# Splitting the first weight block of the projections as well, so that its second unit runs in split passes

## The reference, cut to what matters

```
D_MODEL = 1024; SEQ = 256
(dq, dk, dv, dz, da, db, aq, ak, av, gate_dn, gate_da) = split_columns(xn @ w_in[layer], IN_WIDTHS)
...
q, kc, vc, ks, vs, kw, vw, gl = jnp.split(h @ w_in, cuts, axis=-1)      # NSA
return o @ w_out                                                        # NSA, out of the mixer
...
q, f, i, g = jnp.split(h @ w_in, [HGRN_F_DIM, 2 * HGRN_F_DIM, 2 * HGRN_F_DIM + D_MODEL], axis=-1)   # HGRN2
return o.reshape(b, t, D_MODEL).astype(h.dtype) @ w_out                 # HGRN2, out of the mixer
```

## The kernel before

| call | starts near | units |
|---|---|---|
| first input projection (DeltaNet) | 23 us | 3 blocks feature, 2 token (the last 16 columns wide) |
| second input projection (dilated attention) | 250 us | 6 feature, 3 token |
| NSA in | 1210 us | 6 token (the last 48 columns wide) |
| NSA out (`out_projection`) | 1429 us | 2 token |
| HGRN in | 1809 us | 4 feature, 4 token |
| HGRN out (`out_projection`) | 1994 us | 2 token |

## Time and profile before

### The profile page before, as it was taken

One profiled execution on the slowest core, in us unless ns is written; L12 is line 12 of the kernel. 1 busy time (PEld: TensorE's weight loads), 2 busy tenths in 40 slices (PEclk: granted clock), 3 DMA queues, 4 the chain that ended last, 5 costly groups with the idle time before them and its releaser, 6 DMA issues. The chain is left out here.

```text
span 2366.2 us, 27792 instructions
## 1 busy us (share of the span) xinstructions
PE 2097.6 (89%) x10752; PEld 1413.5 (60%) x10752; DVE 1420.5 (60%) x2421; ACT 610.1 (26%) x1010; POOL 464.9 (20%) x402
## 2 busy tenths in 40 slices
PE   7889998998997777777789898899999978899998
PEld 6679897774542222222257885566775866566584
DVE  5455553557888888555574466433666667443394
ACT  1411102422111111000010231333652052233372
POOL 1032000104443333334312001100011033100000
PEclk9889999999999999999998899999999999999999
DMA  5830664539999999999957101889996532589997
GB/s 206 305 108 1 215 214 147 213 108 419 393 421 421 421 422 421 421 421 418 398 191 213 41 1 47 338 352 355 394 377 241 200 137 73 208 348 351 352 409 283
DMA packets 142432, 650.98 MB, mean 275 GB/s; under 512 B 17976, under 2 KB 22736, under 8 KB 97084
## 3 DMA queue, kind: packets, MB, share of 16 engines
q1 hardware_dynamic: 94012, 354.09, 39.6%
q0 software_dynamic: 46336, 291.93, 30.2%
q10 hardware_dynamic: 1952, 3.18, 0.5%
HBM read 642.46 MB, written 16.85 MB: 279 GB/s over the span
## 5 line engine op out<-in xcount | busy, mean ns | idle before, releaser
L1840 PE MATMUL psum<-peer_uv_rows,peer_weight_diagonal 128*128 128x512 f32 x932 | 453.2, 615 | 108.4 <-DVE peer_weight_diagonal L1966 108.1
L1840 PEld LDWEIGHTS psum<-peer_uv_rows,peer_weight_diagonal 128*128 128x128 f32 x932 | 161.8, 190 | 390.6 <-DVE peer_weight_diagonal L1966 264.9
L1973 DVE SCALAR_TENSOR_TENSOR peer_uv_rows<-peer_uv_rows,peer_x 128x1024 f32<-128x1024 f32 x233 | 285.5, 1225 | 143.6 <-DMA peer_uv_rows<-peer_uv,peer_index 141.3
L1794 POOL DMA_INDIRECT peer_uv_rows<-peer_uv,peer_index x233 | 241.8, 1038 | 448.2 <-PE psum L1840 332.0
L147 DVE TENSOR_TENSOR moe_weight_parts<-weight_ring,moe_weight_parts 128x2048 fp32r<-128x2048 f32 x80 | 182.6, 2290 | 156.4 <-ACT moe_weight_parts L2858 156.0
L1873 ACT ACTIVATE peer_gelu<-peer_dots 128x1 f32<-128x1 f32 x256 | 51.5, 202 | 548.7 <-DVE peer_uv_rows L1973 497.4
L2858 ACT ACTIVATE moe_weight_parts<-weight_ring 128x2048 fp32r<-128x2048 f32 x80 | 152.1, 1911 | 38.0 <-DMA weight_ring<-moe_w 26.1
L153 PE MATMUL psum<-moe_weight_parts,moe_block_x_parts 128*128 128x512 f32 x352 | 142.6, 405 | 11.7 <-DVE moe_block_x_parts L147 7.2
L154 PE MATMUL psum<-moe_weight_parts,moe_block_x_parts 128*128 128x512 f32 x352 | 139.6, 397 | 0.0
L155 PE MATMUL psum<-moe_weight_parts,moe_block_x_parts 128*128 128x512 f32 x352 | 139.4, 396 | 0.0
L2977 POOL DMA_INDIRECT h_t<-moe_tokens,moe_block_tokens x30 | 36.9, 1232 | 498.5 <-PE psum L2676 411.0
(11 more groups left out here) (565 smaller groups left out, 3996.8 us busy)
## 6 DMA issues: line engine op xcount, KB each, us to landing
weight_ring<-moe_w SPq DMA_DIRECT2D x76, 2048.0 KB, 10.3
weight_ring<-ada_w SPq DMA_DIRECT2D x24, 2048.0 KB, 9.2
moe_weight_ring_end<-moe_w SPq DMA_DIRECT2D x20, 2048.0 KB, 12.3
weight_ring<-w_in SPq DMA_DIRECT2D x17, 2048.0 KB, 9.4
weight_ring<-hgrn_w_in SPq DMA_DIRECT2D x8, 2048.0 KB, 9.5
moe_results<-moe_block_out POOLq DMA_DIRECT2D x26, 512.0 KB, 10.3
weight_ring<-nsa_w_in SPq DMA_DIRECT2D x5, 2048.0 KB, 7.9
weight_ring<-peer_wq SPq DMA_DIRECT2D x4, 2048.0 KB, 8.1
```

The lines of the kernel that those rows point to most:

```text
L1794: nc.gpsimd.indirect_dma_start(buffer(t), None, S.dram["peer_uv"], bass.IndirectOffsetOnAxis(ap=experts[:, t:t + 1], axis=0)).then_inc(row ...
L1840: last = nc.tensor.matmul(S.ps[:, 2 * a + c, :], diag[:, t % 4, :], v_rows(t)[:, c * BANK:(c + 1) * BANK], start=(i == 0), stop=(i == PICK ...
L1973: nc.vector.scalar_tensor_tensor(u_rows(t), u_rows(t), 1.0, x2[:, t // PICKS, :], ALU.mult, ALU.mult, accum_out=dots[:, t:t + 1]).then_inc ...
```

## The change

Block 0 keeps its first unit plain and runs its second unit (i = 1) split. PE's waits for the split parts move there: for `split_made` 1 and 2 and for `x_split` 1 and 2 at k = 0 and k = 4 of unit 1. DVE parts block 0 ahead of block 1. If unit 1 is a feature unit, only the columns that it uses are parted (`first = width // 2`), so an instruction is 128x4x256; otherwise the whole block is. The counts of `masked` and `split_made` are two higher for every later block, and as block 0 now has room in `wp` too, `split_block(2)` waits for `spent` 1.

```diff
                 def product(out, k, lhs_part, rhs_part, fresh):
-                    if not with_parts or b == 0:
+                    if not with_parts or i == 0:
                         return nc.tensor.matmul(out, lhs_part(lhs, w), rhs_part(lhs, w), start=(k == 0), stop=(k == K - 1))
                     if fresh and k % (K // 2) == 0:
-                        pe.wait_ge(split_made, 2 * b + k // (K // 2) - 1)
-                        if b == 1:
+                        pe.wait_ge(split_made, 2 * b + k // (K // 2) + 1)
+                        if b == 0:
                             pe.wait_ge(x_split, k // (K // 2) + 1)
...
-                    fresh = w is None
+                    fresh = w is None or i == 1
...
-                    if b >= 3:
+                    if b >= 2:
                         dve.wait_ge(spent, b - 1)
+                    first = width // 2 if b == 0 and units[1][0] == "feature" else 0
                     for h in range(2):
-                        part = half(h, k * width)
-                        high_part(nc, high[:, part], w[:, part]).then_inc(masked, 1)
-                        dve.wait_ge(masked, 2 * b + h - 1)
-                        low_part(nc.vector, low[:, part], w[:, part], high[:, part]).then_inc(split_made, 1)
+                        part = lambda y: y[:, 0:k * width].rearrange("p (k n) -> p k n", k=k)[:, half(h, k), first:width]
+                        high_part(nc, part(high), part(w)).then_inc(masked, 1)
+                        dve.wait_ge(masked, 2 * b + h + 1)
+                        low_part(nc.vector, part(low), part(w), part(high)).then_inc(split_made, 1)
...
                     if b == 1:
                         dve.wait_ge(spent, 1)
-                    dve.wait_ge(split_made, 2 * b)
+                    dve.wait_ge(split_made, 2 * b + 2)
                     dve.sem_inc(S.w.used, 1)
                 if with_parts:
+                    split_block(0)
                     split_block(1)
```

## The result

| | kernel before | changed kernel |
|---|---|---|
| timed runs, median | 2369.58 us (20 runs) | 2376.52 us (20 runs) |
| lowest to highest | 2365.91 to 2373.06 | 2370.47 to 2383.86 |
| ratio, 95% interval | | 1.0030 [1.0022, 1.0038] |
| span of the profiled execution | 2366.2 us | 2369.7 us |

The change makes the kernel slower by 7 us, 0.3%. The profiled execution of the changed kernel was one of its quick ones: 2371.5 us in all, 1.8 us more than its span and 5.0 under the median. With the same 1.8 us on top, the profiled execution of the kernel before took about 2368.0 us (an estimate), 1.6 under its median. So the two spans differ by 3.5 us only, and a comparison of the two traces can explain the six calls, but not all of the 7 us; the last experiments are about that.

What follows compares the result with a forecast made beforehand. PE was taken to set each call's end, with DVE close behind and stretched by POOL. Gains of 0.14, 1.16 and 0.17 against losses of 1.81, 2.07 and 1.8 made +4.2 us on 2370.98, so 2375.2 us, range 2370 to 2381.

Steps and rivals of the forecast that it cites:

- the 0.2% bound: About 0.2% (4.7 us) is what a measurement can tell from no change; the forecast, 0.18% slower, lay within it.
- the likeliest single case: The main forecast, slower but staying within 0.2% of the kernel before; chance 0.44.
- PE's side: Six calls: a plain unit becomes split, saving 1.16 us per feature call and 1.43 per token call, 7.8 if PE never waits.
- DVE's side: Extra splitting on DVE: 6.93 us per token call, 3.72 us for the half block in feature calls.
- rival 3: Feature calls: narrow split saves nothing, CAST of 4x256 taking 1.22 us; 2377.2 us, or 2381.7 with both at full length; chance 0.06.
- The turns with POOL: DVE and POOL block each other, so POOL adds 4.3 us to DVE's chain in whichever order they go.
- Rival 1: DVE is in time: POOL's 4.3 us don't lengthen the chain, no call waits, 7.8 us gained, 2363.2 us; chance 0.10.
- The waits: PE waits for DVE's parts: three per token call (1.6 to 1.9, then twice 0.7 us), one in first call and HGRN in.
- NSA out: Token call: unit 3's mover starts at 1455.62 instead of 1453.55, 2.07 us lost.
- Rival 2: Clock falls in the token calls' new waits, each of three calls paying 1.7 us; 2380.3 us; chance 0.13.
- Rival 4: The waits don't come about, PE or DVE starting otherwise in token calls; gains and losses near nothing, 2371 us; chance 0.04.
- the sum: Six calls: -0.14 - 1.16 - 0.17 + 1.81 + 2.07 + 1.8 = +4.2 us, later stages passing it on unchanged.

Runs made afterwards that it cites:

- the last experiments: Four kernels repeated on another chip (changed kernel 1.0045, feature calls alone 1.0015), then waits padded into the kernel before (0.9999) and decay-table loads moved first in the changed kernel (1.0029).
- both series: The first runs, and a second set of four kernels run together on another chip: kernel before against itself 1.0007, changed kernel 1.0045.

## Why the prediction was right, and where it wasn't

The time, 2376.52 us, lies in the range, 1.3 us over the forecast of 2375.2. But the kernel before measured 2369.58 this time and not 2370.98, so the loss was 6.9 us where +4.2 was forecast: slower by more than the 0.2% bound, where the likeliest single case was just within it.

**PE's side** held: 6.91 to 5.75 in the second call, with no wait, because DVE starts on the half block as soon as block 0 is there, while block 1 is still loading.

**DVE's side** held. On the line between the two known widths the half block had 3.72 us; the third and fourth of its instructions in the second call, away from POOL, run from 255.96 to 257.81, 1.85 us a half where 1.86 was read off the line:

```profile
255.96 0.68 DVE L142 CAST project_weight_parts<-weight_ring 128x1024 fp32r<-128x1024 f32 x1
256.67 1.23 DVE L147 TENSOR_TENSOR project_weight_parts<-weight_ring,project_weight_parts 128x1024 fp32r<-128x1024 f32 x1
257.81 1.22 DVE L142 CAST project_weight_parts<-weight_ring 128x2048 fp32r<-128x2048 f32 x1
```

With this rival 3 is out: CAST takes 0.68 and not 1.22.

**The turns with POOL** held: 4.3 us in whichever order. The second and third instruction in NSA in pay 2.07 and 2.17 beyond the 2.29 and 1.22 that they take alone. In the first call, where the narrow instructions go first, TENSOR_TENSOR at 24.00 pays nothing and the two behind it 2.2 and 2.0. The run without POOL's work shows the cause by taking it away. Rival 1 was right in what follows from a shorter chain (3 us less was its deciding point, and with 4.2 less nothing waits), and wrong in that this kernel isn't there: POOL does lengthen the chain.

**The waits** came where they were said to be, eleven of them. The profile gives 1.45, 0.54 and 0.40 us where 1.6 and twice 0.7 were worked out, but the two count differently. The matmuls ahead follow each other every 0.23 us and are shown as 0.39 long, so PE's pace is interrupted for 0.16 us more than the idle time in the brackets: 1219.61 - 1217.78 - 0.23 = 1.60 for the first, some 0.7 and 0.56 for the others. Only the third is short, by 0.14, because the slow start behind one wait is taken out of the next and the prediction counted it only behind the last. The end isn't touched by this, because only the last wait sets it: 1226.54 + 0.11 for the slow start + 8.16 + 0.22 = 1235.03, where the mover stands.

**NSA out** was mis-sized by 0.25: +2.07 against +1.82. I took the end of DVE's chain in the kernel before, 1437.83 + 2.29, as given, but there DVE began 0.3 us after ScalarE. Its first instruction before, then after:

```profile
1428.92 1.23 DVE L142 CAST project_weight_parts<-weight_ring 128x2048 fp32r<-128x2048 f32 x1 [0.61 <-DVEq L1355]
```
```profile
1427.38 1.23 DVE L142 CAST project_weight_parts<-weight_ring 128x2048 fp32r<-128x2048 f32 x1 [0.32 <-PEq L1357]
```

In the changed kernel it began 0.02 us after ScalarE. An engine's own start at a stage belongs to the measurement, not to the chain.

**Rival 2** is out. The clock in the three stretches with the new waits, of NSA in, NSA out and HGRN out:

```profile
1216.00:1226.00 10.00, 8.02 (x34) 5.79 (x32) 9.90 (x6) 0.04 (x1) 0.14 (x1) 1.00 0.00 0
1435.00:1445.00 10.00, 8.02 (x34) 5.86 (x32) 9.90 (x6) 0.00 (x0) 0.23 (x1) 1.00 0.00 0
2003.00:2013.00 10.00, 7.61 (x32) 5.33 (x31) 9.90 (x7) 0.00 (x0) 0.00 (x0) 1.00 0.00 0
```

PE stood for a fifth to a quarter of these stretches and was granted 1.00 throughout, and so it was to the end of the three calls. **Rival 4** is out too: the waits came.

**What the sum left out** stands in the last sentence before it, "All later stages begin when the call ends, so gains and losses pass on". It puts everything outside the six calls at nothing, and there the timed runs lost some 3 us more than the calls did. By the line through all runs of both series some 2.5 us go with a lower mean clock, and 1.3 us don't and have no known place but for 0.3. Those belong to the small load that lands late in the convolution stage, which was in no term either; of its 1 us only 0.3 are left at the stage's end: from the start of the first call to the start of the stage behind the convolution it is 87.85 us before and 87.80 after, so most of that call's 0.16 is gone. The range covered all this, as "the spread of the runs", without any of it being foreseen. That the time came within 1.3 us of the forecast is luck in part: the sum was 2.7 us short, and the kernel before came out 1.4 us quicker than in its first three runs.

## What to carry to other kernels

Before moving work onto an engine that seems to have time, add up its whole chain at the place in question, with the stretching by the engine with which it takes turns, and compare each half's end with the moment at which the consumer wants it. In a token call here 6.9 us of new work met 4.0 us of slack (the chain ended at 1221.45, and a PE without waits would want the last part at 1225.4), and a saving of 1.43 us per call became a loss of 1.82. The same change pays once the chain is shortened by giving part of it to an engine that doesn't take turns with it (7.8 us of possible gain, some 6 in the calls and 5 in all realised). And before reading a difference of a few microseconds, set the mean granted clock of the runs beside their times, and follow a delay to the end of its stage before it is counted.

## What the runs showed of the hardware

- **Turns between VectorE and GpSimd move, but don't shrink.** With narrow instructions first (0.69 and 1.23 us), DVE's next two took 2.85 and 3.26 where 0.68 and 1.23 are their own lengths: 4.2 us, as for wide ones (4.36 and 3.39 for 2.29 and 1.22).
- **ScalarE stays out of it.** Three casts of 1.9 us on ScalarE, reading the same block, left DVE's four subtractions at 13.16 us for 4 x 2.29 and the GpSimd share.
- **A small load's landing isn't constant.** The same 4 KB load, issued by GpSimd, took 2.7 us in the kernel before and 3.6 to 4.0 with the feature calls changed, the first of which ends 5 us before that stage; with only the counts of waiting instructions changed, 3.0. The cause stays open.
- **The spread of the runs goes with the mean granted clock.** Over nine kernels 0.01 of it went with 10 us of 2370 (5 to 13.5 in single kernels); a stage whose first 10 us had 0.83 instead of 1.00 took 1.69 us longer.
